# A decoder step on one core: the inverse roots reach the partitions by a transpose instead of a product

## The reference

```python
def rmsnorm(x, g):
    xf = x.astype(jnp.float32)
    y = xf * lax.rsqrt(jnp.mean(xf * xf, axis=-1, keepdims=True) + RMS_EPS)
    return (y * g.astype(jnp.float32)).astype(x.dtype)
...
        h = rmsnorm(x, p['norm_mix_pre'][i]) * (1 + sc1) + sh1
        ...
        x = x + g1 * rmsnorm(o, p['norm_mix_post'][i])
        h = rmsnorm(x, p['norm_ffn_pre'][i]) * (1 + sc2) + sh2
        o, buf = conv_ffn(h, ffn_prev[i], p['ffn_w_in'][i], p['ffn_conv_w'][i], p['ffn_conv_b'][i], p['ffn_w_out'][i])
        new_ffn.append(buf)
        x = x + g2 * rmsnorm(o, p['norm_ffn_post'][i])
```

## Time and profile before

| | us |
|---|---|
| median of 3 runs | 2841.78 (2841.56 to 2842.68) |
| the profiled execution, own time | 2835.91 |
| its span | 2834.1 |
| PE busy | 2679.9 (95%) |
| VectorE busy | 1199.2 (42%) |
| ScalarE busy | 864.0 (30%) |
| GpSimd busy | 124.1 (4%) |
| all 16 transfer engines, mean rate | 117 GB/s |

### The profile page before, as it was taken

The page is one execution under the profiler, slowest core; times in us unless marked ns, Lnnn a source line. Parts: engine busy times, 40 slices in busy tenths (PEclk is TensorE's granted clock), DMA queues, the critical chain, the costliest instruction groups (busy, mean ns, idle before and its releaser), DMA issues.

```text
span 2834.1 us, 39971 instructions
## 1 busy us (share of the span) xinstructions
PE 2679.9 (95%) x17488; PEld 2495.1 (88%) x17488; DVE 1199.2 (42%) x1849; ACT 864.0 (30%) x1359; POOL 124.1 (4%) x183
## 2 busy tenths in 40 slices
PE   5899999899999999997999999987899999999997
PEld 3788999899999999997966777657899999999997
DVE  3522236533333335654463444325743333334553
ACT  3311123322121224543233554424422221224342
POOL 1000000000000000000001001100000000000000
PEclk7999999899999999998998999988999999999998
DMA  9565232221112156553000034614312111226653
GB/s 346 213 232 214 77 108 82 76 72 61 60 61 67 60 166 202 173 163 106 16 15 27 21 132 184 254 73 167 117 53 66 62 60 60 70 66 196 202 173 112
DMA packets 320847, 330.71 MB, mean 117 GB/s; under 512 B 14349, under 2 KB 297330, under 8 KB 310877
## 3 DMA queue, kind: packets, MB, share of 16 engines
q1 hardware_dynamic: 299089, 205.48, 23.3%
q0 software_dynamic: 21584, 122.67, 11.3%
HBM read 282.85 MB, written 45.48 MB: 116 GB/s over the span
## 4 chain that ended last, share of the span: by engine, by line
PE 85%; DVE 8%; DMA 3%; ACT 2%; issue 1%; POOL 0%; DVEq 0%; SPq 0%; ACTq 0%; POOLq 0%
PE ps L1992 16%; PE ps L1994 15%; PE ps L1993 15%; PE ps L2027 6%; PE ps L2029 6%; PE ps L2028 6%; PE ps L1861 4%; PE ps L2313 2%; PE ps L2286 2%; PE ps L1870 1%; DVE ss_x L1343 1%; DVE o_sb L1403 1%; DVE xc L1408 1%; PE ps L1908 1%; PE ps L2354 1%
## 5 line engine op out<-in xcount | busy, mean ns | idle before, releaser
L1992 PE MATMUL ps<-h_hi,w_hi 128*128 128x344 f32 x2832 | 914.1, 323 | 30.3 <-DVE h_lo L1383 30.3
L1993 PE MATMUL ps<-h_lo,w_hi 128*128 128x344 f32 x2832 | 909.8, 321 | 0.0
L1994 PE MATMUL ps<-h_hi,w_lo 128*128 128x344 f32 x2832 | 909.4, 321 | 0.0
L1992 PEld LDWEIGHTS ps<-h_hi,w_hi 128*128 128x128 f32 x2832 | 537.9, 190 | 38.8 <-DVE h_lo L1383 31.0
L1994 PEld LDWEIGHTS ps<-h_hi,w_lo 128*128 128x128 f32 x2832 | 537.2, 190 | 0.0
L1993 PEld LDWEIGHTS ps<-h_lo,w_hi 128*128 128x128 f32 x2832 | 536.6, 189 | 0.0
L1260 DVE TENSOR_TENSOR w_lo<-w_raw,w_hi 128x1024 fp32r<-128x1024 f32 (+1 forms) x278 | 325.6, 1177 | 326.6 <-ACT w_hi L837 325.9
L837 ACT ACTIVATE w_hi<-w_raw 128x1024 fp32r<-128x1024 f32 (+1 forms) x278 | 281.9, 1019 | 418.4 <-DMA w_raw<-in_ffn_w_out 161.4
L2027 PE MATMUL ps<-act_hi,w_hi 128*128 128x344 f32 x832 | 268.9, 323 | 23.4 <-DVE act_lo L1433 16.9
L2029 PE MATMUL ps<-act_hi,w_lo 128*128 128x344 f32 x832 | 268.0, 322 | 0.0
L2028 PE MATMUL ps<-act_lo,w_hi 128*128 128x344 f32 x832 | 267.4, 321 | 0.0
(11 more groups left out here) (297 smaller groups left out, 2950.6 us busy)
## 6 DMA issues: line engine op xcount, KB each, us to landing
w_raw<-in_ffn_w_out SPq DMA_DIRECT2D x96, 512.0 KB, 4.0
w_raw<-in_ffn_w_in SPq DMA_DIRECT2D x88, 512.0 KB, 3.7
mod_late<-in_mod_w SPq DMA_DIRECT2D x24, 1536.0 KB, 10.1
w_raw<-in_ffn_w_out SPq DMA_DIRECT2D x48, 384.0 KB, 3.4
act_d<-g_sb POOLq DMA_DIRECT2D x52, 344.0 KB, 3.1
xc<-x_d POOLq DMA_DIRECT2D x12, 1376.0 KB, 6.5
x_d<-xc POOLq DMA_DIRECT2D x9, 1376.0 KB, 5.0
mod_raw<-in_mod_w SPq DMA_DIRECT2D x8, 1536.0 KB, 23.6
```

The costliest lines, as they stand in the source:

```text
L1992: pe.matmul(o, w_hi[k.slot][:, t, :], h_hi[:, t, up_cols(c)], start=t == 0, stop=False)
L1993: pe.matmul(o, w_hi[k.slot][:, t, :], h_lo[:, t, up_cols(c)], start=False, stop=False)
L1994: ins = pe.matmul(o, w_lo[k.slot][:, t, :], h_hi[:, t, up_cols(c)], start=False, stop=t == KD - 1)
```

## The change

`spread` no longer calls a matmul but `trans`, with the same column as the weight; `trans` takes the identity of 86 by 86, as before. Calls, operands, shapes, output, waits and semaphores are the same, and so is every other instruction. The new instructions carry the line of `trans`, 1861; lines below 1908 are one less.

```diff
             def spread(out, k0):
 
                 for t in range(4):
-                    ins = pe.matmul(out[:, t * RB:(t + 1) * RB], t_inv[:, k0 + t:k0 + t + 1].to_broadcast([RB, P]),
-                                    ident[0:RB, 0:RB], start=True, stop=True, skip_group_check=True)
+                    ins = trans(out[:, t * RB:(t + 1) * RB], t_inv[:, k0 + t:k0 + t + 1].to_broadcast([RB, P]))
                 return ins
```

## The result

| | before | changed |
|---|---|---|
| median, us | 2841.67 (4 runs, 2837.58 to 2842.68) | 2819.24 (4 runs, 2817.42 to 2821.43) |
| profiled execution, own time | 2835.91 | 2817.42 |
| its span | 2834.1 | 2815.6 |

The ratio is 0.9924, with a 95% interval of 0.9907 to 0.9941: the change saves 22.4 us by the medians, 16.8 to 26.4 by the interval. The two profiled executions lie 18.5 us apart.

The account below looks back on a forecast made before the run. The prediction took TensorE to bound the kernel, with 85% of the chain. Savings of 10.8 in mid-stream, 3.7 at stage ends and 3.3 in the latent stage made 17.8 us, from 2841.78 to 2824.0; range 2820.5 to 2831.5.

Parts of the forecast that it names:

- The spreads are on the path, in TensorE's stream: Spreads stand between products in TensorE's in-order stream, or VectorE waits for them at stage ends; 1% of the span.
- The cost of a turn of 86 columns: Each turned call in a spread was put at 0.073 us at full clock, 0.146 at half, scaled by moving columns.
- The rival with 0.109: A turn of 86 columns in a spread costs as much as one of 128; 2827.7 us, chance 0.11.
- the 0.055: Cost in us of a turned call by the skill's factor of 4, from 2 x 0.11; whole saving then 19.8 us.
- Mid-stream, 20 x 0.54 = 10.8: Each of 20 spreads amid streams of products takes 0.28 us instead of 0.82 to the next product; 10.8 us saved.
- VectorE's chain moves along, so the waits stay as they are: Behind mid-stream spreads, VectorE's chain and TensorE's products both move forward half a microsecond, so TensorE's waits for roots don't grow.
- The rival that the gain turns into waits: Part of the mid-stream and latent-stage saving is given back in waits and clock; 11.9 us saved, 2829.9, chance 0.10.
- Stage ends 3.7: Four spreads at stage ends, where VectorE and the first product wait behind them, save 3.7 us together.
- Latent stage 3.3: Three spreads in a row in the latent stage fall from 5.15 to 1.85 us; 3.3 saved, 1.8 as lower end.
- Start: nothing: The three first spreads save nothing, being covered by VectorE's work on the modulation and the first tiles.
- The clock doesn't fall in mid-stream for the turns: Turned spreads in mid-stream keep full clock, as a stretch of 22 turns did; so no half-clock products behind them.
- Slower: Rival: the clock falls behind each of 20 mid-stream spreads, costing 42 us against 17.8 saved; 2866 us, chance 0.02.

Follow-up runs that it names:

- narrow turns: All spreads turned, with four extra turns of a 64-column weight ahead of each four, against the changed kernel; one time, 2826.6 us.
- the rounded kernel: Spreads as one-pass products again, inverse roots and identity in fp32r instead of turns; ratio 0.9961 against the kernel before, 11.1 us saved.
- mid: Only the 20 mid-stream spreads turned, the other ten left as products; ratio 0.9966 against the kernel before, 9.7 us saved.
- three comparisons: The changed kernel, without further edit, measured three times against runs of the kernel before; ratios 0.9924, 0.9927 and 0.9936.
- ends: First three, four stage-end and three latent-stage spreads turned, the 20 in mid-stream left as products; ratio 0.9981 against the kernel before, 5.4 us saved.

## Why the prediction was right, and where its range was wrong

- *The spreads are on the path, in TensorE's stream.* Right, and shown: doubling them costs 0.89 us at each of 20 places, and turning them gains 0.56 to 0.61 at 19, before what waits take back.
- *The cost of a turn of 86 columns*, 0.073 us by scaling with the moving columns (0.146 at half clock). Right: 0.073 to 0.075, and 0.143. That the weight doesn't set it is shown by the narrow turns. That the weight sets a product's pass is shown by `token_sums`, and the rounded kernel agrees: one pass remained and was no faster than before. The rival with 0.109 fell. So did the 0.055 that the prediction worked out from the factor of 4 of the Trainium skill ("TensorE: Matmul & The Clock Gate", Terms). Measured, the factor is 3.1 for 86 columns (0.224 us in two passes to 0.073). The prediction's remark that it is only about half held a turn of 128 moving columns against a product of 86, which are not the same shape.
- *Mid-stream, 20 x 0.54 = 10.8.* 11.3 by the records (the next product follows the last turn by 0.03, not 0.06), 9.7 with 6.8 to 12.5 by the time of `mid`.
- *VectorE's chain moves along, so the waits stay as they are.* Right at most places, wrong at three. VectorE starts 0.58 earlier behind a spread, and the waits for roots in front of a spread stay at 15 and 22.8 us. But in front of three `token_sums` TensorE waits longer, 1.7 to 2.2 us together in the three profiles of the changed kernel; at the third of them VectorE, now earlier, waits 0.97 to 1.18 us for a transfer of x for which it did not wait before. The rival that the gain turns into waits (11.9 saved) fell as a size in all three comparisons, but its mechanism is there at these places. The later fall of the clock at two stage ends, which the prediction did not have, gives back 2.1 to 2.7 us of the same sign as the saving and covers it; at the third stage end an earlier fall takes 0.95. That these parts nearly cancel, so that the whole saving stays near the sum of the terms, is luck.
- *Stage ends 3.7.* 3.5 by the records. *Latent stage 3.3.* 3.45, and the clock's return went with the products in the kernel that had only this part.
- *Start: nothing.* Right. In the three profiles of the changed kernel and in that of `ends`, TensorE waits 5.27 us for its first product where it waited 4.10, and the lead up to that product grows by 0.04: the shorter spreads end in a longer wait. The 2.9 us at the start of the changed kernel's profile came before its first spread.
- *The clock doesn't fall in mid-stream for the turns.* Right as a mechanism: behind none of the spreads does a stretch of half clock begin that isn't behind a wait. Slower did not happen.
- *The range, 2820.5 to 2831.5.* This is the step that failed, in the prediction's words the "one microsecond of the medians' own spread". It put the ends of the unknown spacing at 2822.0 and 2827.7 and allowed that microsecond beyond them (2820.5 is in fact 1.5 below 2822.0). It was read off three runs that happened to lie 1.1 us apart. Single executions of the kernel before spread over 9.5 us, two profiles of one changed kernel differ by 7.8, and the savings of the three comparisons lie 3.4 apart by their ratios (18.2 to 21.6). With 3 to 4 us on either side the range would have held the first result, 2819.24, and the later 2819.62; 2820.51 lies just inside the range as stated. How much of the 4.6 us between 17.8 and 22.4 is scatter and how much a mis-sized sum can't be told from three comparisons; the terms themselves measured 18.3. The profile had given the warning: its execution was 5.9 us from the median, and the prediction used that number without drawing a width from it.

## What to carry to other kernels

Where a float32 product only moves data (one operand is an identity), do it in the transpose mode: here a call went from two passes of 0.112 us to one of 0.073, and in the stream that TensorE bounds most of it came back. Read costs from start to start and the saving place by place, and look at the waits in front of the neighbouring work too, not only at those in front of the changed instructions: where the other engine's chain meets a transfer that isn't earlier too, the gain ends in a wait. But take the width of a forecast from how far single executions lie apart, the profiled one included, and not from a median of three.

## What the runs showed of the hardware

- A one-pass fp32r product with a weight of 128 columns keeps the spacing of an f32 pass, 0.112 us at full and 0.215 at half clock with 86 moving columns; its weight load is 190 ns, that of a turn with the same weight 137. The gain is not from the number of passes alone.
- An f32 product pass goes by its weight's columns when few columns move: eight passes took 0.63 us with a weight of 86 columns and 0.82 with 128, at full clock; at half clock 8 and 86 moving columns gave 0.22 and 0.21 a pass.
- A turn's spacing doesn't change when its weight goes from 128 to 64 columns: 0.073 us with 86 moving columns.
- A weight that is one column read 128 times shows no extra cost in a turn: its load is 137 ns against a median of 140 for the turns of the cached pages with a weight of 128 columns, and the spacing of 0.073 is 0.109 x 86/128.
- After the latent spreads, the products of one and the same kernel ran at half clock for 1.8, 4.7 and 4.7 us in three executions. Such phases and waits of other lengths make up the 7.8 us between two executions of one kernel.
